# Four column groups for modulation rows and sums of squares in a three-layer float32 network on one core

## What is computed

```python
def _layer_norm(x, g, b):
    mu = jnp.mean(xf, axis=-1, keepdims=True)
    var = jnp.mean(jnp.square(xf - mu), axis=-1, keepdims=True)
    return ((xf - mu) * lax.rsqrt(var + EPS) * g + b).astype(x.dtype)

def _adaln(cond, w_mod, b_mod):
    m = jax.nn.silu(cond) @ w_mod + b_mod
    return jnp.split(m, 3, axis=-1)          # shift, scale, gate

def _post_norm(x, y, gate, g, b):
    return _layer_norm(ALPHA * x + gate * y, g, b)
...
# layer 0, for x with c and for ctx with c_ctx
sh, sc, gt = _adaln(c, ab_w_mod[j], ab_b_mod[j])
h = x * (1.0 + sc[:, None]) + sh[:, None]
y = _ab_mixer(h, ...)                        # in-projection, pool, gating unit, out-projection
x = _post_norm(x, y, gt[:, None], ab_ln_g[j], ab_ln_b[j])
# layer 1: the same with cd_w_mod, a Fourier mixer and latent attention (over ctx and x)
# layer 2: rms norm, convolution and sparse attention, memory attention, and 128 x 128
#          experts of which 128 per token are gathered; a last rms norm
```

## Time and profile before

| | us |
|---|---|
| median of three runs (2675.37 to 2677.31) | 2675.55 |
| time of the profiled execution | 2673.3 |
| its span, first to last instruction | 2671.4 |
| TensorE busy | 2374.0 (89%) |
| VectorE busy | 1432.6 (54%) |
| ScalarE busy | 682.5 (26%) |
| GpSimd busy | 611.7 (23%) |

### The profile page before, as it was taken

The page is one execution under the profiler, slowest core; times in us unless marked ns, Lnnn a source line. Parts: engine busy times, 40 slices in busy tenths (PEclk is TensorE's granted clock), DMA queues, the critical chain, the costliest instruction groups (busy, mean ns, idle before and its releaser), DMA issues.

```text
span 2671.4 us, 23577 instructions
## 1 busy us (share of the span) xinstructions
PE 2374.0 (89%) x7882; PEld 1247.0 (47%) x7882; DVE 1432.6 (54%) x3726; ACT 682.5 (26%) x1640; POOL 611.7 (23%) x566
## 2 busy tenths in 40 slices
PE   6999999989999999899989898888888878788776
PEld 2456554444645456448845444444334334343332
DVE  0010222026532667521577777787777777677765
ACT  2000012015511124512234222233222232222222
POOL 0002000001000000000144444444444444344441
PEclk9999999989999989899999999999999999899999
DMA  8101332000021110013299999999999999999996
GB/s 332 63 32 67 154 138 114 32 32 1 5 98 63 67 64 32 33 63 126 98 400 397 421 421 421 421 413 422 421 422 421 422 420 421 422 421 421 421 421 276
DMA packets 83943, 657.20 MB, mean 246 GB/s; under 512 B 9410, under 2 KB 9698, under 8 KB 11378
## 3 DMA queue, kind: packets, MB, share of 16 engines
q0 software_dynamic: 75760, 549.06, 49.7%
q1 hardware_dynamic: 8066, 106.65, 10.2%
HBM read 653.58 MB, written 2.10 MB: 245 GB/s over the span
## 4 chain that ended last, share of the span: by engine, by line
PE 56%; DMA 31%; DVE 9%; issue 2%; ACT 2%; POOL 0%; SPq 0%; DVEq 0%; POOLq 0%; PEldq 0%; ACTq 0%
DMA arena<-in_peer_uv,newton 29%; PE psum L573 21%; PE psum L1182 11%; PE psum L643 3%; DMA arena<-in_weights 2%; PE psum L1059 2%; DVE arena L2242 2%; PE psum L623 1%; PE psum L1124 1%; PE psum L1151 1%; PE psum L739 1%; PE psum L789 1%; PE psum L995 1%; PE psum L797 1%; PE psum L810 1%
## 5 line engine op out<-in xcount | busy, mean ns | idle before, releaser
L1182 PE MATMUL psum<-arena 128*128 128x512 f32 x2048 | 975.5, 625 | 205.6 <-ACT arena L1578 203.1
L2242 DVE CUSTOM_DVE_ANT_0 arena<-arena 128x1024 f32<-128x1024 f32 x512 | 620.8, 1224 | 284.7 <-DMA arena<-in_peer_uv,newton 280.8
L2400 POOL DMA_INDIRECT arena<-in_peer_uv,newton x512 | 569.3, 1112 | 835.6 <-PE psum L1182 708.3
L1182 PEld LDWEIGHTS psum<-arena 128*128 128x128 f32 x2048 | 397.4, 200 | 694.8 <-issue 690.2
L573 PE MATMUL psum<-arena 128*128 128x512 f32 (+2 forms) x1440 | 548.7, 542 | 10.9 <-DVE arena L1758 3.6
L573 PEld LDWEIGHTS psum<-arena 128*128 128x128 f32 (+1 forms) x1440 | 270.1, 189 | 287.2 <-issue 275.6
L1267 ACT ACTIVATE arena<-psum 128x512 f32<-128x512 f32 (+9 forms) x328 | 169.5, 535 | 696.8 <-PE psum L573 308.5
L1578 ACT ACTIVATE arena<-ident,newton 128x128 f32<-128x128 f32 x512 | 177.8, 394 | 266.9 <-DVE newton L2251 263.4
L1569 ACT ACTIVATE arena<-arena 128x2 f32<-128x2 f32 (+1 forms) x258 | 52.5, 203 | 660.5 <-DVE arena L2242 660.5
L1151 PE MATMUL psum<-arena 128*128 128x256 f32 x480 | 122.3, 380 | 0.9 <-DMA arena<-in_weights 0.4
L1151 PEld LDWEIGHTS psum<-arena 128*128 128x128 f32 x480 | 91.0, 190 | 62.5 <-issue 54.7
(11 more groups left out here) (307 smaller groups left out, 2086.4 us busy)
## 6 DMA issues: line engine op xcount, KB each, us to landing
arena<-in_weights SPq DMA_DIRECT2D x48, 2048.0 KB, 9.0
arena<-in_peer_uv,newton POOLq DMA_INDIRECT x512, 24.7
arena<-in_xin SPq DMA_DIRECT2D x1, 3072.0 KB, 28.5
arena<-in_dft_l POOLq DMA_DIRECT2D x1, 2048.0 KB, 16.3
arena<-in_cmp_w POOLq DMA_DIRECT2D x1, 2048.0 KB, 7.7
out<-arena SPq DMA_DIRECT2D x4, 512.0 KB, 11.8
arena<-in_pool_band POOLq DMA_DIRECT2D x1, 1280.0 KB, 12.7
arena<-in_fnet_w POOLq DMA_DIRECT2D x1, 1024.0 KB, 23.1
```

Of the source, the lines that this page charges most:

```text
L1182: ins = mm(bank(j_y[t][q]), DIAG[i % 4], ROW[ROW_PLACE[i]][:, D + 512 * q:D + 512 * q + 512], start=first, stop=last)
L2242: v.tensor_tensor_reduce(out=u, in0=u, in1=HNT[ITEM_TILE[i // 16]][:, :], scale=1.0, scalar=0.0, op0=ALU.mult, op1=ALU.add, accum_out=DOTS ...
L2400: g.indirect_dma_start(out=ROW[ROW_PLACE[i]][:, :], out_offset=None, in_=a["peer_uv"], in_offset=bass.IndirectOffsetOnAxis(ap=IDX[:, n, e: ...
```

## The change

- **Rows.** `modulation_rows` sends feature chunk k to column group k % 4: the stationary operand has 32 columns (two of the condition and 30 zeros), the moving one all 512 columns of the block, and the result lies in partitions 32q to 32q+31. There are 8 products per block, and each group holds a partial sum of two chunks. ScalarE copies the whole bank, 128 partitions by 512.
- **Columns.** A chunk's column is no longer a transpose but a product of the 128x128 piece with `sel`, a 128x2 selector that adds the four groups' partial rows.
- **Sums of squares.** `norm_sum` gives way to `norm_parts` (chunk k in column group k % 4, 32 columns of ones), a copy by ScalarE into `PART`, and `norm_total`, one product with `FOLD` that adds the groups. It is used for both parts behind layer 0, for the memory tokens, and twice behind layer 1. Two later uses of `norm_sum`, in layer 2, stay.
- **Order.** `cd_mod_lo` has four blocks (shift and scale) and `cd_mod_hi` two (gate). One of the four stands behind the pool weights, three behind the gating products, in front of the output projection. Their columns are made in two steps, and VectorE adds the gate's later. Behind layer 1, the first sum of squares stands in front of the first positions sum, and the second positions sum behind the third set of memory keys.
- **ScalarE** copies the partial sums: behind layer 0 it does the second part's squares and copy in front of the first part's root.
- VectorE builds `sel` and `FOLD` at the start and clears the padded condition.

```diff
-BLOCKS = [("ab_mod", 4), ("ab_in", 5), ("ab_gate", 2), ("cd_mod_lo", 3), ("ab_out", 2), ("cd_mod_hi", 3), ("cd_in", 4), ("cd_out", 2), ("mem_k_lo", 1), ("in2", 5),
+BLOCKS = [("ab_mod", 4), ("ab_in", 5), ("ab_gate", 2), ("cd_mod_lo", 4), ("ab_out", 2), ("cd_mod_hi", 2), ("cd_in", 4), ("cd_out", 2), ("mem_k_lo", 1), ("in2", 5),
...
-        cond = sm(16).rearrange("p (k s) -> p k s", s=2)
+        cond = extra[:, 0:8 * 32].rearrange("p (k s) -> p k s", s=32)
+        PART = extra[:, 0:512]
+        sel = sm(2)
+        FOLD = sm(P)
...
                     for k in range(KC):
-
-                        for half in range(2):
-                            ins = mm(bank(jobs[b], 256, 256 * half, 64 * half, 64 * half + 2), cond[:, k, :],
-                                     w[:, 2 * half:2 * half + 2, k, :], start=(k == 0), stop=(k == KC - 1))
+                        q = k % 4
+                        ins = mm(bank(jobs[b], 512, 0, 32 * q, 32 * q + 32), cond[:, k, :], w[:, :, k, :],
+                                 start=(k < 4), stop=(k >= 4))
...
-                    ins = nc.tensor.transpose(bank(job, 2, 2 * c), mod_rows[0:2, c * P:(c + 1) * P], ident[0:2, 0:2])
+                    ins = mm(bank(job, 2, 2 * c), mod_rows[:, (first + c) * P:(first + c + 1) * P], sel[:, :], start=True, stop=True)
...
+            def norm_parts(job, src, lo, n, kc, ready, r0):
+
+                claim(pe, job)
+                for k in range(kc):
+                    pe.wait_ge(ready, r0 + k + 1)
+                    q = k % 4
+                    ins = mm(bank(job, n, 0, 32 * q, 32 * q + 32), ones[:, 0:32], src[:, k, lo:lo + n],
+                             start=(k < 4), stop=(k >= kc - 4))
+                done(ins, job)
+
+            def norm_total(job, part, n):
+
+                read_out(pe, [part])
+                claim(pe, job)
+                done(mm(bank(job, n), FOLD[:, :], PART[:, 0:n], start=True, stop=True), job)
...
             modulation_rows("ab_gate", j_gate_rows, range(2))
-            modulation_rows("cd_mod_lo", j_mod_cd_rows[0:3], range(3))
...
-            modulation_columns(j_gate_rows, j_gate[0], MODR_GATE, 8)
+            modulation_rows("cd_mod_lo", j_mod_cd_rows, range(1))
+            modulation_columns(j_gate_rows, j_gate[0], MODR_GATE, 0, 8)
...
+            modulation_rows("cd_mod_lo", j_mod_cd_rows, range(1, 4))
...
-            modulation_rows("cd_mod_hi", j_mod_cd_rows[3:6], range(0, 3))
-            norm_sum(j_ln_ab[1][0], SQ, 0, L, KC, S["squared"], 0)
-            modulation_columns(j_mod_cd_rows, j_mod_cd[0], MODR_CD)
-            norm_sum(j_ln_ab[1][1], SQ, L, LC, KC, S["squared"], KC)
-
+            modulation_rows("cd_mod_hi", j_mod_cd_rows[4:6], range(2))
+            modulation_columns(j_mod_cd_rows[0:4], j_cd_lo[0], MODR_CD, 0, 16)
+            norm_parts(j_part_ab[0], SQ, 0, L, KC, S["squared"], 0)
+            modulation_columns(j_mod_cd_rows[4:6], j_cd_hi[0], MODR_CD, 16, 8)
+            norm_total(j_ln_ab[1][0], j_part_ab[0], L)
+            norm_parts(j_part_ab[1], SQ, L, LC, KC, S["squared"], KC)
+            norm_total(j_ln_ab[1][1], j_part_ab[1], LC)
...
-                    norm_sum(j_rms_mem[0], MEMSQ, 0, LC, KC, S["mem_sq"], 0)
+                    norm_parts(j_part_mem[0], MEMSQ, 0, LC, KC, S["mem_sq"], 0)
+                if b == 2:
+                    norm_total(j_rms_mem[0], j_part_mem[0], LC)
...
             memory_keys(0, 0, KC)
+            norm_parts(j_part_cd[0], SQ, 0, L, KC, S["squared"], 16)
+            norm_total(j_ln_cd[1][0], j_part_cd[0], L)
...
             positions_sum(0)
-            norm_sum(j_ln_cd[1][0], SQ, 0, L, KC, S["squared"], 16)
             memory_keys(1, 0, KC)
+            norm_parts(j_part_mix[0], SQ, 0, L, KC, S["squared"], 24)
+            norm_total(j_rms_mix[0], j_part_mix[0], L)
+            memory_keys(2, 0, KC)
             positions_sum(1)
-            norm_sum(j_rms_mix[0], SQ, 0, L, KC, S["squared"], 24)
-            memory_keys(2, 0, KC)
             memory_keys(3, 0, KC)
...
-            for s, (lo, n) in enumerate(SEGS):
-                squares(SQ, X, lo, n, KC, S["centered"], KC * s)
-            for b in range(3, 5):
+            squares(SQ, X, 0, L, KC, S["centered"], 0)
+            for b in range(4, 6):
                 modulation_rows_out(j_mod_cd_rows[b], b, MODR_CD)
-            for b in range(5, 6):
-                modulation_rows_out(j_mod_cd_rows[b], b, MODR_CD)
+            part_out(j_part_ab[0], L)
+            squares(SQ, X, L, LC, KC, S["centered"], KC)
+            full(act, j_ln_ab[1][0])
+            part_out(j_part_ab[1], LC)
             root(j_ln_ab[1][0], RS1[:, 0:L], L)
```

More of the change, by code:

```diff
@@ L396, in build @@
         j_gate_rows = J.turn(2)
-        j_mod_cd_rows = J.turn(3)
         j_poolw = J.turn(8)
+        j_mod_cd_rows = J.turn(1)
         j_gate = J.turn(1)
         j_sgu = J.turn(8)
+        j_mod_cd_rows += J.turn(3)
         mean_ab = J.turn(2)
-        j_ab_out = J.turn(16, [j[0] for j in mean_ab])
-        j_mod_cd_rows += J.turn(2, [j[0] for j in mean_ab])
-        j_ln_ab = [mean_ab, J.turn(2)]
-        j_mod_cd_rows += J.turn(1)
-        j_mod_cd = J.turn(1)
+        means = [j[0] for j in mean_ab]
+        j_ab_out = J.turn(16, means)
+        j_mod_cd_rows += J.turn(2, means)
+        j_cd_lo = J.turn(1, means)
+        j_part_ab = J.turn(1, means)
+        j_cd_hi = J.turn(1, means)
+        j_ln_ab = [mean_ab, J.turn(1, means)]
+        j_part_ab += J.turn(1, means)
+        j_ln_ab[1] += J.turn(1, means)
         j_cq = J.turn(2)
@@ L410, in build @@
         j_fin = J.turn(4)
+        j_part_mem = J.turn(1)
+        j_fg = J.turn(4)
         j_rms_mem = J.turn(1)
-        j_fg = J.turn(4)
         j_dg = J.turn(4)
@@ L438, in build @@
         j_mk = J.turn(1)
+        j_part_cd = J.turn(1)
+        j_ln_cd = [mean_cd, J.turn(1)]
         j_pos = J.turn(1)
-        j_ln_cd = [mean_cd, J.turn(1)]
+        j_mk += J.turn(1)
+        j_part_mix = J.turn(1)
+        j_rms_mix = J.turn(1)
         j_mk += J.turn(1)
         j_pos += J.turn(1)
-        j_rms_mix = J.turn(1)
-        j_mk += J.turn(2)
+        j_mk += J.turn(1)
         j_ca = J.turn(4)
@@ L1271, in modulation_rows_out, with part_out @@
             def modulation_rows_out(job, b, dst):
-                for half in range(2):
-                    col = b * 512 + 256 * half
-                    copy_out(job, dst[0:2, col:col + 256], 256, p0=64 * half, p1=64 * half + 2, free=(half == 1), lo=256 * half)
+                copy_out(job, dst[:, b * 512:(b + 1) * 512])
+            def part_out(job, n):
+                copy_out(job, PART[:, 0:n], n)
             act.wait_ge(S["small_loaded"], 48)
-            fn(cond[:, :, :].rearrange("p k s -> p (k s)"), vc("cond", 0, 16), ACT.Silu).then_inc(S["cond_ready"], 1)
+            act.wait_ge(S["const_ready"], 1)
+            fn(cond[:, :, 0:2], vc("cond", 0, 16).rearrange("p (k s) -> p k s", s=2), ACT.Silu).then_inc(S["cond_ready"], 1)
             for b in range(4):
@@ L1316, in root @@
                 fn(dst, NEWTON[:, 0:n], ACT.Abs_reciprocal_sqrt).then_inc(S["rooted"], 1)
-            for b in range(3):
+            for b in range(4):
                 modulation_rows_out(j_mod_cd_rows[b], b, MODR_CD)
-            for s, (lo, n) in enumerate(SEGS):
-                squares(SQ, X, lo, n, KC, S["centered"], KC * s)
-            for b in range(3, 5):
+            squares(SQ, X, 0, L, KC, S["centered"], 0)
+            for b in range(4, 6):
                 modulation_rows_out(j_mod_cd_rows[b], b, MODR_CD)
-            for b in range(5, 6):
-                modulation_rows_out(j_mod_cd_rows[b], b, MODR_CD)
+            part_out(j_part_ab[0], L)
+            squares(SQ, X, L, LC, KC, S["centered"], KC)
+            full(act, j_ln_ab[1][0])
+            part_out(j_part_ab[1], LC)
             root(j_ln_ab[1][0], RS1[:, 0:L], L)
@@ L1352, in _ @@
                 copy_out(j_fin[c], F_IN[:, c, :])
+            part_out(j_part_mem[0], LC)
             for jobs, dst in ((j_fg, FG), (j_dg, DG)):
@@ L1404, in _ @@
             squares(SQ, X, 0, L, KC, S["centered"], 16)
+            part_out(j_part_cd[0], L)
             copy_out(j_mk[0], MK[:, 0, :], LC)
@@ L1410, in _ @@
                     .then_inc(S["squared"], 1)
+            part_out(j_part_mix[0], L)
             copy_out(j_mk[1], MK[:, 1, :], LC)
@@ L1708, in _ @@
             dve.wait_ge(S["small_loaded"], 48)
+            dve.wait_ge(S["const_ready"], 1)
+            link(v.reduce_sum(sel[:, :], ident[:, :].rearrange("p (q s) -> p s q", s=32)[:, 0:2, :], axis=AX))
+            v.tensor_scalar(FOLD[:, :], ones[:, :], sel[:, 0:1], None, ALU.mult).then_inc(S["fold_ready"], 1)
             modulation(j_mod_ab[0], "ab_b_mod", mod_ab, S["mod_ab_ready"], 16)
```

16 lines of the change are left out of this document (10 added, 6 removed).

## The result

The changed kernel takes 2656.38 us (median of 4 runs, 2654.24 to 2658.97) against 2676.01: ratio 0.9926, 95% interval 0.9909 to 0.9944. Its profiled execution has a span of 2654.3 us, 17.1 less than that of before; 17.4 less was forecast, and 2658 for the median. The medians lie 19.6 apart, because the profiled execution of before (2673.3) was faster than its median. The sum came out right, its terms less so: up to layer 2 the gain is 14.5 us; a stretch in layer 2 in which nothing is edited gave another 3.8, and 1.2 was lost in the last stage.

A forecast was written before the change was run, and what follows sets the result against it. The gather (DMA engines at 0.99) bounds the last half, and TensorE, nearly always busy, what precedes it. Gains of 7.05 + 5.2 + 2.25 + 2.9 = 17.4 us take the median from 2675.55 to 2658; range 2652 to 2671.

The forecast's parts named there:

- start: First modulation blocks and columns, up to TensorE's feed at 37.55 us: weights hide both changes; gain 0, at worst 0.5 lost.
- A: 261.40 to 297.70 us, modulation blocks to gating products before the output projection: output starts at 290.65, 7.05 us gained.
- B: 382.7 to 412.4 us, behind layer 0's chunk sums: the wait for weights goes; 5.2 us gained, between 8.35 and 2.
- C: Sum over the memory tokens at 475.82 us, between busy neighbours: 3.53 becomes 1.28 us, 2.25 gained.
- D: 790.4 to 828.2 us, TensorE almost without gaps: 2.9 us gained, between 4.5 and 0.5, one low-clock stretch charged.
- The main question: Whether four column groups run together in a modulation block: 1.87 us taken, 3.6 with two abreast, 7.0 with none.
- what comes last is new: the first output block: In A, its slot is freed at 282.45 us; 8.2 us of refill lets the output start at 290.65.
- The ideal 8.35: Gain in B at the full clock, in us; 3.1 charged for two low-clock stretches left 5.2.
- what leaves TensorE's path brings the whole gather forward by as much: Before 1340 us, time saved on TensorE shifts the gather equally, unless something else comes last there.
- Rival 1: Modulation blocks: only two passes overlap, a block stays at 3.62 us; gain 5, time 2670.5; chance 0.12.
- rival 3: Modulation blocks: four groups do not overlap, a block is 7.0 us; 32 us slower, 2708; chance 0.05.
- Rival 2: Thin stretches keep TensorE at 1.2 GHz in B, D and following loops' starts; gain about 7, time 2668; chance 0.08.

The follow-up runs named there:

- before_again: The kernel before, unchanged, profiled once more; 2676.45 us (1 run).
- pairs: The changed kernel with neighbouring feature chunks in one column group (q = k // 2 instead of k % 4); 2660.15 us, ratio 0.994.
- one_group: The changed kernel with all eight products of a modulation block in the first column group; 2707.77 us (1 run) against 2676.53.
- rows_only: The kernel before with only the four-group rows and product columns; block order, sums of squares and ScalarE's order as before; 2679.57 us, ratio 1.0007.
- old_rows: The changed kernel with rows on two column groups, transposed columns and copies in their old form; 2659.32 us, ratio 0.9935.
- old_norms: The changed kernel with whole sums of squares in the five places and no partial copies; 2665.04 us, ratio 0.9964.
- before_x1: The kernel before with one needless product in front of the first projection of layer 2; 2676.26 us, ratio 1.0002.
- before_x2: The kernel before with two needless products in front of the first projection of layer 2; 2676.99 us (1 run).
- both: The changed kernel with root_first's edit and the second scale/shift block moved directly behind the first; 2652.07 us, ratio 0.9913.
- root_first: The changed kernel with the first part's root in front of the second part's partial-sum copy on ScalarE, behind layer 0; 2661.98 us, ratio 0.9942.

## Why the prediction was right, and where its terms were off

| place | forecast gain | measured gain |
|---|---|---|
| start, to the modulation blocks of A | 0 | -1.0 |
| A | 7.05 | 6.50 |
| output projection of layer 0 | 0 | -0.3 |
| B, with the first loop behind it | 5.2 | 4.05 |
| C, with the loops around it | 2.25 | 2.0 |
| D | 2.9 | 3.3 |
| layer 2, unchanged | 0 | 3.8 |
| last stage and the rest | 0 | -1.2 |
| span | 17.4 | 17.1 |

Of the start's -1.0, the kernel before alone shows 0.8 from one execution to the next: in before_again A begins at 262.18 instead of 261.40.

**The main question** was answered right: four groups run side by side, a block takes 1.92 us (1.87 forecast), and what the earlier trace rows showed for two products holds for four (window of 60 ns above, pairs, and 7.03 us in one_group). The Trainium skill's rule ("TensorE: Matmul & The Clock Gate", packing small matmuls) that matmuls start strictly in program order would, by an estimate from two passes abreast, have given 3.6; the trace does not agree with it for float32 products.

**A.** The step "what comes last is new: the first output block" held, 8.4 us after the slot was given back where 8.2 were forecast. Of the missing half microsecond, 0.4 lies in the steps ahead of that release (blocks follow each other at 2.25 us, not 2.17) and the rest in the refill.

**B.** The mechanism held: no wait for weights, the table load directly before the root, and from the total's end to the in-projection 7.4 us where the steps gave 7.6. The ideal 8.35 shrank to 5.88 within the stage, since the partial sum and the gate columns ran slow (1.35 and 0.4 us) and 0.7 of waits stood ahead of the columns; another 1.8 went in the loop behind. I had charged 3.1 for the clock and it took 3.6.

**D.** The gain of 3.3 against 2.9 hides two errors. The norm's chain ran as forecast (last square at 19.8 us behind the chunk sum). On TensorE the low clock cost 3.4 us (positions sum and keys), twice the one stretch charged. But I had TensorE wait about 3 us for those squares, and the slow keys ended at 799.22, just as the last square was done (799.02), so most of the 3.4 took the place of that wait.

**The total** owes its closeness to luck. The terms, summed as measured up to D, give 14.5 and not 17.4; an unchanged stretch of layer 2 gave 3.8 more, at a clock of 0.93 instead of 0.89, and the last stage took 1.2 back. Without the stretch the gain would have been 13.3, which is still inside the range. The step that failed is "what leaves TensorE's path brings the whole gather forward by as much": that was true of the work, and left out that an unchanged stretch can take several microseconds more or less from one profile to another, with its mean clock. What decides that stays open.

**The rivals.** Rival 1 (two abreast) and rival 3 (none) fell with the block time. Rival 3's 2708 us and the 2707.77 of one_group agree only by chance: in one_group the partial sums of squares still overlap, and 9 us were lost at the start, which I had taken as hidden. Rival 2 named a real mechanism at a smaller size. What I did not list is how much hangs on the order: without the order and the partial sums the faster rows bring nothing (rows_only), and without four groups for the rows the rest keeps all but 3 us (old_rows). No run has the new order alone, so how the rest divides between it and the partial sums is known only by stages (old_norms).

## What to carry to other kernels

Small products that write different groups of 32 output partitions overlap, in float32 as well, in both orders of the chunks that were tried; but look first at what comes last. Here the time saved on rows turned into waits for weights until the blocks were also moved to where their slots come free in time. Folding partial sums costs a copy, a product and perhaps a place in another engine's queue: it paid where TensorE was the bound (C, D), and not in a latency chain (B). Judge an edit of 1 to 5 us by stages that contain it, and look at the clock of all other stages before crediting the total to it.

## What the runs showed of the hardware that I had not expected

- Passes of float32 products in different column groups start within 20 ns of each other although earlier passes of the program still wait; four groups give 3.7 times one (1.92 against 7.03 us).
- The same 813 passes of layer 2 took 139.5 to 144.4 us in the profiles (mean clock 0.93 at 140.3, 0.89 at 144.2); D of the kernel before took 37.8 or, in before_x1 and before_x2, 41.1.
- The gather stage, with the same work in all kernels, took 1331 to 1337 us in eight of nine profiles (before, after and the kernels from rows_only to both), and 1341 in the ninth, at 408 instead of 411 GB/s. This is more than most edits here are worth. The ninth is the slowest run of root_first (2669.68): of the 13.6 us between its span and the changed kernel's, 8.6 are the gather and 5.0 lie ahead of it:

```profile
1326.40:2667.80 1341.40, 1127.27 (x2850) 541.52 (x2850) 971.27 (x2613) 370.30 (x986) 559.47 (x505) 0.95 0.99 408
1316.80:2648.20 1331.40, 1119.01 (x2850) 538.01 (x2850) 970.76 (x2613) 370.24 (x986) 564.07 (x505) 0.96 0.99 411
```

The first row is root_first, the second is both.
